# A delta-rule slot rearranged: the block substitution split around k S's part, VectorE's and ScalarE's rows in another order, GpSimd's long operations moved, G ahead of k'y

## The chip, the cores and the metric

The program runs on 1 core of a Trainium2 chip. The metric is the device time in microseconds of that core, from a run of the whole program; less is better. Before the change it is 2587.37 us (median of 3 runs, 2584.19 to 2587.85).

## The reference, cut to what matters

One step of a hybrid encoder layer: a projection, a gated delta rule with 8 heads (the part touched here), latent attention with 8 heads, and an output projection. 1024 prompt tokens and 32 sample tokens are processed, all in float32. The delta rule per chunk, with state `s`:

```python
lmat = where(strict, (k * beta) @ k.T * decay, 0)
tmat = triangular_solve(lmat + eye, eye)          # unit lower triangular
u = tmat @ (v * beta);  w = tmat @ (k * beta * exp(g))
attn = (q @ k.T) * decay
v_new = u - w @ s
o = (q * exp(g)) @ s + attn @ v_new
s = s * exp(g_last) + (k * exp(g_last - g)).T @ v_new
o_g = rmsnorm(o) * gdn_norm_w * silu(z_g)
```

## The kernel before, in words

The program has four stages that follow each other, each its own block: `project`, `delta_rule`, `attend`, `project_out`. Only `delta_rule` (span from about 1191 to 1626 us) is changed. It works on chunks of 128 tokens: chunks 0 to 7 are the prompt, chunk 8 (`LAST`) the sample, with its own state.

Each engine has its own instruction stream, written out by hand, and waits on semaphores (`Ledger.wait`). All streams run over the same slots: `each_slot` calls `slot(c)` for c from -2 to 9. In slot c the engines work on three chunks at once:

- chunk c+2, the early part: transposes of q and k (`qT`, `kT`), norms (`sse`, then `rs`, a power on GpSimd, then five small VectorE operations in `coefficients`: `kb`, `nlam`, `nle`, `sqc`, `sq2`), the decay matrix `D` from `gm_hi` and `gm_lo` (GpSimd, `growth`), its exponential `dL` and weighted copy `dLb` (ScalarE), the Gram matrix `G` (TensorE) and from them `lmat` (VectorE, `lower_products`, called L below).
- chunk c+1, the triangular solve: `substitute` on VectorE makes the inverses of 16x16 diagonal blocks, row by row: for i from 1 to 15 a product `m{i}` of `Lrep` and `x` and a reduction `x{i}`, each waiting for the one before. ScalarE expands `x` into `Y` (`Yx`), TensorE turns it (`X`), and `P4_`, `Y4_`, `X4_`, `P5_`, `Y5_`, `X5_`, `P6`, `Y6` join the blocks with the masks `C4` and `C5` (GpSimd).
- chunk c, the state: TensorE makes `kS`, `qS`, `y`, `dS`, `Ay`; VectorE adds into `R`, `qe`, the state `S` and the output `o`; ScalarE copies `y` and squares `o` (`osq`). GpSimd makes the decayed state `Sd`. Chunk c-1 is normalised (`orr`, `on` on GpSimd) and turned (`oT`), gated (`mix`) and stored.

`Lrep` is `lmat`'s diagonal blocks, repeated. It goes through DRAM: SyncE's `bounce(c+2)` waits for L, stores 8 blocks, waits for them, and loads 1024 KB back.

TensorE's results go to PSUM in pairs of banks. `PHASES` gives the order of TensorE's phases in a slot, and four pairs are handed out in turn: a phase takes the pair of the phase four places ahead of it, and `free` waits until that one's reader (`FREED`) is done.

`x13`, `m14` and so on are the rows of the substitution; in the rows of a trace their operations are told apart by size (`m{i}` has 8*i elements a partition, `x{i}` reads 8*(i+1)). `gdn_C` is C4 or C5, `gdn_o<-gdn_b,gates_eg` is qe, `gdn_o<-gdn_o,gdn_orr` is on.

Of the kernel before, what the change touches and what calls it, by code (L numbers as in the profile page):

```python
# [16 lines left out]
EPS = 1e-6  # L17
# [503 lines left out]
def delta_rule(nc, a, d, cols, ident, out, g_all, g_hi, g_lo, beta, eg, egl, edl):  # L521
# [4 lines left out]
    with ExitStack() as ctx:  # L526
# [134 lines left out]
        @block.gpsimd  # L661
        def _(pool):
            pool.memset(mhalf[:], -0.5).then_inc(set_up, 1)
            pool.memset(S[:, 0], 0.0).then_inc(set_up, 1)
            pool.wait_ge(set_up, 2)
            pool.wait_ge(consts_in, 16 * CONSTS)

            def mask(c, k, name, C):

                if k == 0:  # L670
                    DVE.wait(pool, c, "L1")
                PE.wait(pool, c - 1, f"P{4 + k}_1")
                POOL.done(pool.tensor_tensor(C[:], lmat[:, c % 2], level[:, k:k + 1, :].to_broadcast(full), ALU.mult), c, name)

            def growth(c, name, gm, g):

                PE.wait(pool, c - 1, "D1")
                POOL.done(pool.tensor_tensor(gm[:], lower[:, None, :].to_broadcast(full), g[:, c, :, None].to_broadcast(full), ALU.mult), c, name)

            def slot(c, live):  # L680
                if live(c + 1):
                    mask(c + 1, 0, "C4", C4)
                if live(c - 1):
                    DVE.wait(pool, c - 1, "orr")
# [8 lines left out]
                if live(c):  # L693
                    DVE.wait(pool, c - 1, "S1")
                    POOL.done(pool.tensor_tensor(Sd[:], S[:, stream(c)], egl[:, c, :, None].to_broadcast(full), ALU.mult), c, "Sd")
                if live(c + 2):
                    DVE.wait(pool, c + 2, "sse")
                    POOL.done(pool.tensor_tensor(rs[:], sse[:], mhalf[:], ALU.pow), c + 2, "rs")
# [12 lines left out]
        def _(act):
# [54 lines left out]
            def slot(c, live):  # L766
# [61 lines left out]
        def _(dve):  # L828
# [40 lines left out]
            def substitute(c, rows):  # L869

                for i in rows:
# [7 lines left out]
                    DVE.done(dve.tensor_reduce(x[:, :, i:i + 1].rearrange("p h o -> p (h o)"), prod[:, :, AT[i]:AT[i] + i + 1], AX.X, ALU.add), c, f"x{i}")  # L879

            def slot(c, live):
                if live(c):
                    POOL.wait(dve, c, "Sd") if c == 0 else None
# [40 lines left out]
                if live(c):  # L924
                    ACTS.wait(dve, c, "osq")
                    DVE.done(dve.tensor_tensor(var[:], oss[:], sq2[:, c], ALU.mult), c, "var0")
                    own(c, "var0")
                    DVE.done(dve.tensor_scalar(var[:], var[:], EPS, None, ALU.add), c, "var")
# [18 lines left out]
        def _(pe):  # L947
# [39 lines left out]
            def slot(c, live):  # L987
# [1130 lines left out]
```

## Time and profile before

| what | value |
|---|---|
| median of 3 runs | 2587.37 us |
| the profiled execution, its own time | 2585.61 us |
| its span | 2583.8 us |
| PE busy in the span | 2347.6 us (91%) |
| DVE, ACT, POOL busy | 1051.7, 746.8, 463.0 us |
| delta rule, slots 0 to 7 | 1269.25 to 1597.95 us of the span |

Times are microseconds from the start of the span. A row of the timeline gives the start, the length and the count of merged instructions; the bracket gives how long the engine sat idle before it and what released it. A slot is counted here from the first weight load of `kS`, and "at 8.2" in a slot means 8.2 us after that.

### The profile page before, as it was taken

To read this page: it belongs to the slowest core of one execution; us is meant where nothing else is said; L and a number is where in the kernel's file an instruction comes from. 1 tells how busy PE (TensorE), PEld (TensorE's weight loads), DVE (VectorE), ACT (ScalarE), POOL (GpSimd) and SP (SyncE) were. 2 spreads that over 40 slices of the span, in tenths; PEclk is the share of its full clock that TensorE was granted. 3 is DMA by queue.
4 is the path that set the end of the run, shared out by engine and by line. 5 is a ranking of instruction groups with operands and counts; after the bars stand their busy time and mean duration, and the time that the engine had idled before them with its cause. 6 is when DMAs were issued, how large, how long until landed. Compare 5 with 4: busy or idle time off the path is not lost. (4 is left out here: it accounts for less than half of the span.)

```text
span 2583.8 us, 37042 instructions
## 1 busy us (share of the span) xinstructions
PE 2347.6 (91%) x15280; PEld 2250.8 (87%) x15280; DVE 1051.7 (41%) x1743; ACT 746.8 (29%) x1860; POOL 463.0 (18%) x287
## 2 busy tenths in 40 slices
PE   6899999999999999995587878698999995999997
PEld 5899999999999999995587877597887874999997
DVE  3321345555545111110456565464444542334343
ACT  4111011111111111103456553323344341343343
POOL 1111222222212211112243543110000000111111
PEclk8999999999999999997799989799999998999999
DMA  5222122222222221213444422534222117858564
GB/s 159 71 75 75 50 75 75 66 67 66 75 75 75 75 75 60 74 50 93 88 91 94 108 51 60 172 125 116 58 59 88 56 43 244 248 144 253 150 186 128
DMA packets 328557, 257.72 MB, mean 100 GB/s; under 512 B 32533, under 2 KB 308326, under 8 KB 323942
## 3 DMA queue, kind: packets, MB, share of 16 engines
q1 hardware_dynamic: 300582, 219.33, 30.4%
q10 hardware_dynamic: 27808, 36.03, 3.8%
q8 instruction: 122, 2.00, 0.3%
q14 instruction: 45, 0.37, 0.0%
HBM read 192.42 MB, written 62.91 MB: 99 GB/s over the span
## 5 line engine op out<-in xcount | busy, mean ns | idle before, releaser
L457 PE MATMUL proj_acc<-proj_hn_hi,proj_w_hi 128*128 128x352 f32 (+1 forms) x2352 | 763.3, 325 | 7.0 <-DVE proj_hn_lo L338 6.0
L457 PE MATMUL proj_acc<-proj_hn_lo,proj_w_hi 128*128 128x352 f32 (+1 forms) x2352 | 755.6, 321 | 0.0
L457 PE MATMUL proj_acc<-proj_hn_hi,proj_w_lo 128*128 128x352 f32 (+1 forms) x2352 | 755.2, 321 | 0.0
L457 PEld LDWEIGHTS proj_acc<-proj_hn_hi,proj_w_hi 128*128 128x128 f32 (+1 forms) x2352 | 440.4, 187 | 8.8 <-issue 6.7
L457 PEld LDWEIGHTS proj_acc<-proj_hn_lo,proj_w_hi 128*128 128x128 f32 (+1 forms) x2352 | 441.3, 188 | 0.6
L457 PEld LDWEIGHTS proj_acc<-proj_hn_hi,proj_w_lo 128*128 128x128 f32 (+1 forms) x2352 | 440.1, 187 | 0.9
L2052 PE MATMUL mixo_acc<-mixo_m_hi,mixo_w_hi 128*128 128x384 f32 (+1 forms) x768 | 253.0, 329 | 31.6 <-DMA mixo_m_lo<-scratch_mix 21.6
L218 POOL TENSOR_TENSOR proj_w_raw<-proj_w_raw,all_cols 128x2048 f32<-128x2048 f32 (+1 forms) x49 | 175.7, 3586 | 420.3 <-DMA proj_w_raw<-in_w_in 420.3
L2052 PE MATMUL mixo_acc<-mixo_m_hi,mixo_w_lo 128*128 128x384 f32 (+1 forms) x768 | 248.7, 324 | 0.0
L2052 PE MATMUL mixo_acc<-mixo_m_lo,mixo_w_hi 128*128 128x384 f32 (+1 forms) x768 | 248.4, 323 | 0.0
L369 DVE TENSOR_TENSOR proj_act_out<-proj_acc,proj_rstd_b 128x352 f32<-128x352 f32 (+1 forms) x75 | 39.1, 524 | 365.9 <-PE proj_acc L457 353.4
L1990 DVE TENSOR_TENSOR mixo_w_lo<-mixo_w_raw,mixo_w_hi 128x2048 fp32r<-128x2048 f32 x48 | 110.0, 2292 | 175.2 <-ACT mixo_w_hi L1956 175.2
L343 DVE TENSOR_TENSOR proj_w_lo<-proj_w_raw,proj_w_hi 128x2048 fp32r<-128x2048 f32 (+1 forms) x49 | 111.5, 2276 | 162.1 <-ACT proj_w_hi L264 162.1
L2052 PEld LDWEIGHTS mixo_acc<-mixo_m_hi,mixo_w_hi 128*128 128x128 f32 x768 | 145.6, 190 | 34.1 <-DVE mixo_w_lo L1990 26.8
L380 DVE SCALAR_TENSOR_TENSOR proj_act_out<-proj_pre,all_cols,proj_act_out 128x1059 f32<-128x1059 f32 x72 | 172.7, 2399 | 2.5
L287 ACT ACTIVATE proj_act_out<-proj_act_out 128x1059 f32<-128x1059 f32 x24 | 26.2, 1090 | 474.6 <-DVE proj_act_out L380 474.6
L2052 PEld LDWEIGHTS mixo_acc<-mixo_m_lo,mixo_w_hi 128*128 128x128 f32 x768 | 145.9, 190 | 0.0
L2052 PEld LDWEIGHTS mixo_acc<-mixo_m_hi,mixo_w_lo 128*128 128x128 f32 x768 | 145.7, 190 | 0.0
L264 ACT CAST proj_w_hi<-proj_w_raw 128x2048 fp32r<-128x2048 f32 (+1 forms) x49 | 92.9, 1896 | 124.6 <-DVE proj_act_out L369 94.1
L365 DVE TENSOR_TENSOR proj_pre<-proj_acc,proj_rstd_b 128x352 f32<-128x352 f32 (+1 forms) x96 | 39.1, 429 | 182.4 <-PE proj_acc L457 179.9
L291 ACT ACTIVATE proj_act_out<-proj_act_out 128x1056 f32<-128x1056 f32 x16 | 17.4, 1087 | 305.0 <-DVE proj_act_out L369 305.0
L1956 ACT CAST mixo_w_hi<-mixo_w_raw 128x2048 fp32r<-128x2048 f32 x48 | 90.9, 1893 | 31.9 <-DMA mixo_w_raw<-in_w_out 31.7
(285 smaller groups left out, 3573.7 us busy)
## 6 DMA issues: line engine op xcount, KB each, us to landing
proj_w_raw<-in_w_in SPq DMA_DIRECT2D x48, 1024.0 KB, 5.7
mixo_w_raw<-in_w_out SPq DMA_DIRECT2D x48, 1024.0 KB, 6.1
scratch_qkv<-proj_act_out ACTq DMA_DIRECT2D x24, 529.5 KB, 2.8
gdn_qkv<-scratch_qkv SPq DMA_DIRECT2D x8, 1536.0 KB, 8.3
gdn_Lrep<-scratch_blocks SPq DMA_DIRECT2D x9, 1024.0 KB
scratch_gate<-proj_act_out ACTq DMA_DIRECT2D x16, 528.0 KB, 2.7
mixo_y<-in_x_prompt SPq DMA_DIRECT2D x8, 1024.0 KB, 9.1
out_y_prompt<-mixo_y SPq DMA_DIRECT2D x8, 1024.0 KB, 5.2
```

The source lines that it names most:

```text
L218: POOL.done(pool.tensor_tensor(w_raw[:, :, 0:n], w_raw[:, :, 0:n], cols[:, 0, R_LN:R_LN + KT][:, :, None].to_broadcast([P, KT, n]), ALU.mu ...
L264: ACTS.done(act.copy(w_hi[:, t % 2, :, 0:n], w_raw[:, :, 0:n]), t, "hi")
L287: ACTS.done(act.activation(act_out[:, b], act_out[:, b], ACT.Silu), j, "silu")
L291: ACTS.done(act.activation(act_out[:, b, 0:T], act_out[:, b, 0:T], ACT.Silu), QKV_TILES + j, "silu")
L343: DVE.done(dve.tensor_tensor(w_lo[:, t % 2, :, 0:n], w_raw[:, :, 0:n], w_hi[:, t % 2, :, 0:n].bitcast(F32), ALU.subtract), t, "lo")
L365: last = dve.tensor_tensor(pre[:, b, first + shift:end + shift], acc[b][c][:, first - NW * c:end - NW * c], rstd_b[:, first:end], ALU.mult)
L369: last = dve.tensor_tensor(act_out[0:n, b, cut(c)], acc[b][c][0:n, 0:NW], rstd_b[0:n, cut(c)], ALU.mult)
L380: DVE.done(dve.scalar_tensor_tensor(y, pre[:, b, n:n + CONV], w[n], y, ALU.mult, ALU.add), j, f"c{n}")
L457: last = pe.matmul(acc[b][c][0:n, 0:NW], w[:, b, k, 0:n], h[:, k, cut(c)], start=(k == 0 and i == 0), stop=(k == KT - 1 and i == 2))
L1956: ACTS.done(act.copy(w_hi[:, i % 2], w_raw[:, i % 2]), i, "hi")
L1990: DVE.done(dve.tensor_tensor(w_lo[:, i % 2], w_raw[:, i % 2], w_hi[:, i % 2].bitcast(F32), ALU.subtract), i, "lo")
L2052: last = pe.matmul(acc[i % 4][:, 0:n], w[:, i % 2, k], h[:, g % 2, k, 0:n], start=(k == 0 and x == 0), stop=(k == KT - 1 and x == 2))
```

## The change

Every operation stays; only places and waits move.

- VectorE: rows 1 to 7 of the substitution (chunk c+1) go ahead of `R`(c), rows 8 to 13 behind it, then `sse`, rows 14 and 15, `qe`, the coefficients. `o` goes ahead of L. The variance goes behind the first four additions of the solve. `S` waits for `Sd` once.
- GpSimd: the order in a slot is `rs`(c+2), `on`(c-1), C5(c+1), `gmh` and `gml`(c+3), (the memset), `Sd`(c+1), `mix_lo`(c-1), `orms`(c), C4(c+2). `on` also waits for row 15 of the substitution. `growth` and `Sd` are now made one slot earlier than they are used; chunk 0's `growth` stands ahead of the slots.
- ScalarE: `Yx` goes ahead of `dLb`; the copies of X and P4_ go ahead of the squares of o.
- TensorE: G goes ahead of dS. With `PHASES` changed in the same way, X takes the banks that G had (and so waits for L) and P4_ those that dS had (and waits for S); before it was the other way round.

```diff
-        PHASES = ["kS", "qT", "kT", "qS", "y", "D", "dS", "G", "Ay", "oT", "X", "P4_", "Y4_", "X4_", "P5_", "vT", "Y5_", "X5_", "A", "P6", "aT", "Y6"]
+        PHASES = ["kS", "qT", "kT", "qS", "y", "D", "G", "dS", "Ay", "oT", "X", "P4_", "Y4_", "X4_", "P5_", "vT", "Y5_", "X5_", "A", "P6", "aT", "Y6"]
...
@@ GpSimd
+            def both(c):
+                growth(c, "gmh", gm_hi, g_hi[:].bitcast(F32))
+                growth(c, "gml", gm_lo, g_lo[:])
+
             def slot(c, live):
-                if live(c + 1):
-                    mask(c + 1, 0, "C4", C4)
-                if live(c - 1):
-                    DVE.wait(pool, c - 1, "orr")
-                    POOL.done(pool.tensor_tensor(o[:, (c - 1) % 2], o[:, (c - 1) % 2], orr[:, :, None].to_broadcast(full), ALU.mult), c - 1, "on")
-                if live(c + 2):
-                    growth(c + 2, "gmh", gm_hi, g_hi[:].bitcast(F32))
-                    growth(c + 2, "gml", gm_lo, g_lo[:])
...
                 if live(c + 2):
                     DVE.wait(pool, c + 2, "sse")
                     POOL.done(pool.tensor_tensor(rs[:], sse[:], mhalf[:], ALU.pow), c + 2, "rs")
+                if live(c - 1):
+                    DVE.wait(pool, c - 1, "orr")
+                    if live(c + 1):
+                        DVE.wait(pool, c + 1, f"x{BASE - 1}")
+                    POOL.done(pool.tensor_tensor(o[:, (c - 1) % 2], o[:, (c - 1) % 2], orr[:, :, None].to_broadcast(full), ALU.mult), c - 1, "on")
                 if live(c + 1):
                     mask(c + 1, 1, "C5", C5)
+                if live(c + 3):
+                    both(c + 3)
...
+                if live(c + 1):
+                    DVE.wait(pool, c, "S1")
+                    POOL.done(pool.tensor_tensor(Sd[:], S[:, stream(c + 1)], egl[:, c + 1, :, None].to_broadcast(full), ALU.mult), c + 1, "Sd")
...
+                if live(c + 2):
+                    mask(c + 2, 0, "C4", C4)
+
+            both(0)
             each_slot(slot)
...
@@ ScalarE
+                if live(c + 1):
+                    expand(c + 1)
+                if live(c + 2):
                     DVE.wait(act, c + 2, "nlam")
...
                 if live(c + 1):
-                    expand(c + 1)
+                    PE.wait(act, c, "Y6")
+                    evacuate(c + 1, "X", X)
+                    PE.wait(act, c, "X5_1")
+                    evacuate(c + 1, "P4_", pc)
...
@@ VectorE
             def slot(c, live):
+                if live(c + 1):
+                    substitute(c + 1, range(1, BASE // 2))
                 if live(c):
...
+                if live(c + 1):
+                    substitute(c + 1, range(BASE // 2, BASE - 2))
                 if live(c + 2):
                     norms(c + 2)
+                if live(c + 1):
+                    substitute(c + 1, range(BASE - 2, BASE))
                 if live(c):
...
-                if live(c + 1):
-                    substitute(c + 1, range(1, BASE // 2))
                 if live(c + 2):
                     coefficients(c + 2)
-                if live(c + 1):
-                    substitute(c + 1, range(BASE // 2, BASE))
```

The engines' rows at three places. GpSimd in a middle slot before; the first row is C4 of chunk c+1, the second `on`, the third and fourth `growth` for c+2:

```order
L673 TENSOR_TENSOR gdn_C<-gdn_lmat,gdn_level 128x1024
L685 TENSOR_TENSOR gdn_o<-gdn_o,gdn_orr 128x1024
L678 TENSOR_TENSOR gdn_gm_hi<-gdn_lower,gates_g_hi 128x1024
L678 TENSOR_TENSOR gdn_gm_lo<-gdn_lower,gates_g_lo 128x1024
L695 TENSOR_TENSOR gdn_Sd<-gdn_S,gates_egl 128x1024
L698 TENSOR_TENSOR gdn_rs<-gdn_sse,gdn_mhalf 128x16
L673 TENSOR_TENSOR gdn_C<-gdn_lmat,gdn_level 128x1024
L703 TENSOR_TENSOR gdn_mix_lo<-gdn_mix,gdn_mix_hi 128x1024
L706 TENSOR_TENSOR gdn_orr<-gdn_var,gdn_mhalf 128x8
```

One long operation (C5) stands between `rs` and the wait for ScalarE's `mix_hi`. GpSimd in a middle slot now:

```order
L687 TENSOR_TENSOR gdn_rs<-gdn_sse,gdn_mhalf 128x16
L692 TENSOR_TENSOR gdn_o<-gdn_o,gdn_orr 128x1024
L673 TENSOR_TENSOR gdn_C<-gdn_lmat,gdn_level 128x1024
L678 TENSOR_TENSOR gdn_gm_hi<-gdn_lower,gates_g_hi 128x1024
L678 TENSOR_TENSOR gdn_gm_lo<-gdn_lower,gates_g_lo 128x1024
L703 TENSOR_TENSOR gdn_Sd<-gdn_S,gates_egl 128x1024
L706 TENSOR_TENSOR gdn_mix_lo<-gdn_mix,gdn_mix_hi 128x1024
L709 TENSOR_TENSOR gdn_orr<-gdn_var,gdn_mhalf 128x8
L673 TENSOR_TENSOR gdn_C<-gdn_lmat,gdn_level 128x1024
```

Four long operations follow `rs` now, ahead of the wait for the state in `Sd`. VectorE in the middle of the substitution before, around the five coefficients:

```order
L877 TENSOR_TENSOR gdn_prod<-gdn_Lrep,gdn_x 128x8x7
L879 TENSOR_REDUCE gdn_x<-gdn_prod 128x8
L849 TENSOR_TENSOR gdn_kb<-gdn_rs,gates_beta 128x8
L851 SCALAR_TENSOR_TENSOR gdn_nlam<-gdn_rs,gdn_kb 128x8
L853 TENSOR_TENSOR gdn_nle<-gdn_nlam,gates_eg 128x8
L854 TENSOR_SCALAR gdn_sqc<-gdn_rs 128x8
L856 SCALAR_TENSOR_TENSOR gdn_sq<-gdn_sqc 128x8
L877 TENSOR_TENSOR gdn_prod<-gdn_Lrep,gdn_x 128x8x8
```

The rows 8 to 15 of the substitution stand behind the coefficients, then S, L and o. VectorE from `sse` to S now:

```order
L852 TENSOR_SCALAR gdn_sse<-gdn_ssq 128x16
L884 TENSOR_TENSOR gdn_prod<-gdn_Lrep,gdn_x 128x8x14
L886 TENSOR_REDUCE gdn_x<-gdn_prod 128x8
L884 TENSOR_TENSOR gdn_prod<-gdn_Lrep,gdn_x 128x8x15
L886 TENSOR_REDUCE gdn_x<-gdn_prod 128x8
L915 TENSOR_TENSOR gdn_o<-gdn_b,gates_eg 128x512 x2
L856 TENSOR_TENSOR gdn_kb<-gdn_rs,gates_beta 128x8
L858 SCALAR_TENSOR_TENSOR gdn_nlam<-gdn_rs,gdn_kb 128x8
L860 TENSOR_TENSOR gdn_nle<-gdn_nlam,gates_eg 128x8
L861 TENSOR_SCALAR gdn_sqc<-gdn_rs 128x8
L863 SCALAR_TENSOR_TENSOR gdn_sq<-gdn_sqc 128x8
L922 TENSOR_TENSOR gdn_S<-gdn_Sd,gdn_b 128x512 x2
```

The substitution has ended when the coefficients come; S, o and then L stand behind them.

## Rows read from the trace of the kernel before

**Rows 1.** Groups by line and shape, delta rule: busy us, mean ns | idle before.

```profile
L678 POOL TENSOR_TENSOR gdn_gm_lo<-gdn_lower,gates_g_lo 128x1024 fp32r<-128x1024 f32 x9 | 17.1, 1899 | 0.0
```

**Rows 2.** Windows, slots 0, 3, 5 and 7: length, busy per engine, clock, DMA.

```profile
1269.25:1310.22 40.97, 34.22 (x288) 32.84 (x286) 23.58 (x65) 23.10 (x94) 11.39 (x6) 0.92 0.38 80
...
1394.07:1436.00 41.93, 35.57 (x296) 34.04 (x294) 24.90 (x67) 23.98 (x95) 18.97 (x10) 0.92 0.44 103
...
1478.00:1521.43 43.43, 35.58 (x296) 34.04 (x294) 26.39 (x67) 23.98 (x95) 20.96 (x11) 0.92 0.35 72
...
1563.35:1597.95 34.60, 29.39 (x258) 28.55 (x256) 21.15 (x59) 14.38 (x45) 10.01 (x6) 0.95 0.13 36
```

**Rows 3.** Timeline of slot 3: start, length, engine, line, operation [idle before].

```profile
1395.27 2.16 DVE L889 SCALAR_TENSOR_TENSOR gdn_R<-gdn_b,gdn_nle,gdn_R 128x128 f32<-128x128 f32 x8 [3.49 <-PE gdn_b L970]
...
1400.94 0.17 DVE L845 TENSOR_SCALAR gdn_sse<-gdn_ssq 128x16 f32<-128x16 f32 x1 [3.51 <-ACT gdn_sqT L734]
...
1401.19 2.91 POOL L698 TENSOR_TENSOR gdn_rs<-gdn_sse,gdn_mhalf 128x16 f32<-128x16 f32 x1 [1.87 <-DVE gdn_sse L845]
...
1404.06 2.36 POOL L673 TENSOR_TENSOR gdn_C<-gdn_lmat,gdn_level 128x1024 f32<-128x1024 f32 x1
...
1404.43 2.05 DVE L877 TENSOR_TENSOR gdn_prod<-gdn_Lrep,gdn_x 128x48 f32<-128x48 f32 x1
...
1412.46 1.27 DVE L908 TENSOR_TENSOR gdn_S<-gdn_Sd,gdn_b 128x512 f32<-128x512 f32 x2
...
1413.65 1.28 DVE L867 TENSOR_TENSOR gdn_lmat<-gdn_b,gdn_dLb 128x512 f32<-128x512 f32 x2
...
1415.07 1.57 PEld L976 LDWEIGHTS gdn_b<-all_ident,gdn_Y 128*128 128x128 f32 x8 [5.31 <-ACT gdn_Y L721]
...
1421.08 2.02 PE L970 MATMUL gdn_b<-gdn_pc,gdn_X 128*128 128x128 f32 x16 [0.62 <-ACT gdn_pc L758]
1421.29 0.62 SPq L645 DMA_DIRECT2D gdn_Lrep<-scratch_blocks  x1
...
1433.56 0.16 DVE L942 TENSOR_TENSOR gdn_orr<-gdn_orr,gdn_sqc 128x8 f32<-128x8 f32 x1
```

**Rows 4.** Timeline, projection stage: a long GpSimd operation beside VectorE's first of three.

```profile
340.34 3.61 POOL L218 TENSOR_TENSOR proj_w_raw<-proj_w_raw,all_cols 128x2048 f32<-128x2048 f32 x1
343.89 1.22 POOL L236 COPY proj_pre<-all_cols 128x3 f32<-128x3 f32 x1
...
340.37 4.69 DVE L380 SCALAR_TENSOR_TENSOR proj_act_out<-proj_pre,all_cols,proj_act_out 128x1059 f32<-128x1059 f32 x1
```

**Rows 5.** By source line, that VectorE operation: least, median, greatest ns.

```profile
L380 DVE SCALAR_TENSOR_TENSOR proj_act_out<-proj_pre,all_cols,proj_act_out x72: 1321/1323/4694, 294.6 to 827.1; 128x1059 f32<-128x1059 f32 x72
```

**Rows 6.** Timeline of slot 5, where C5 meets the first coefficient.

```profile
1490.36 2.36 POOL L673 TENSOR_TENSOR gdn_C<-gdn_lmat,gdn_level 128x1024 f32<-128x1024 f32 x1
...
1490.49 2.25 DVE L849 TENSOR_TENSOR gdn_kb<-gdn_rs,gates_beta 128x8 f32<-128x8 f32 x1
```

**Rows 7.** Timeline of slot -1: the first Lrep and an undisturbed substitution.

```profile
1224.61 0.67 SPq L645 DMA_DIRECT2D gdn_Lrep<-scratch_blocks  x1
...
1238.86 0.17 DVE L877 TENSOR_TENSOR gdn_prod<-gdn_Lrep,gdn_x 128x8 f32<-128x8 f32 x1 [16.41 <-DMA gdn_Lrep<-scratch_blocks]
...
1241.96 0.16 DVE L849 TENSOR_TENSOR gdn_kb<-gdn_rs,gates_beta 128x8 f32<-128x8 f32 x1
...
1242.72 0.22 DVE L877 TENSOR_TENSOR gdn_prod<-gdn_Lrep,gdn_x 128x64 f32<-128x64 f32 x1
...
1246.11 0.28 DVE L877 TENSOR_TENSOR gdn_prod<-gdn_Lrep,gdn_x 128x112 f32<-128x112 f32 x1
```

**Rows 8.** The page, DMA issues: KB each, median us from issue to landing.

```profile
gdn_qkv<-scratch_qkv SPq DMA_DIRECT2D x8, 1536.0 KB, 8.3
...
gdn_gate<-scratch_gate SPq DMA_DIRECT2D x8, 512.0 KB, 13.6
```

**Rows 9.** Timeline of slot -1: TensorE's Y4_ of chunk 0.

```profile
1254.33 2.01 PE L970 MATMUL gdn_b<-gdn_pc,gdn_X 128*128 128x128 f32 x16
```

More of the change, by code:

```diff
@@ L570, in delta_rule @@
                      state=two("R", "qe", "S", "o") + ["var0", "var"], scale=["orr"], tail=two("mix"))
-        POOL = Ledger(s, "pool", early=["gmh", "gml", "rs"], solve=["C4", "C5"], state=["Sd", "orms"], tail=["on", "mix_lo"])
+        POOL = Ledger(s, "pool", early=["gmh", "gml", "rs"], solve=["C4", "C5"], decayed=["Sd"], state=["orms"], tail=["on", "mix_lo"])
         consts_in, set_up, rounded, sample_padded, ssm_out = (
@@ L678, in growth @@
                 POOL.done(pool.tensor_tensor(gm[:], lower[:, None, :].to_broadcast(full), g[:, c, :, None].to_broadcast(full), ALU.mult), c, name)
+            def both(c):
+                growth(c, "gmh", gm_hi, g_hi[:].bitcast(F32))
+                growth(c, "gml", gm_lo, g_lo[:])
             def slot(c, live):
-                if live(c + 1):
-                    mask(c + 1, 0, "C4", C4)
+                if live(c + 2):
+                    DVE.wait(pool, c + 2, "sse")
+                    POOL.done(pool.tensor_tensor(rs[:], sse[:], mhalf[:], ALU.pow), c + 2, "rs")
                 if live(c - 1):
                     DVE.wait(pool, c - 1, "orr")
+                    if live(c + 1):
+                        DVE.wait(pool, c + 1, f"x{BASE - 1}")
                     POOL.done(pool.tensor_tensor(o[:, (c - 1) % 2], o[:, (c - 1) % 2], orr[:, :, None].to_broadcast(full), ALU.mult), c - 1, "on")
-                if live(c + 2):
-                    growth(c + 2, "gmh", gm_hi, g_hi[:].bitcast(F32))
-                    growth(c + 2, "gml", gm_lo, g_lo[:])
+                if live(c + 1):
+                    mask(c + 1, 1, "C5", C5)
+                if live(c + 3):
+                    both(c + 3)
                 if c + 3 == LAST:
@@ L692, in slot @@
                     pool.memset(qkv[:, LAST % 3, :, DEC:], 0.0).then_inc(sample_padded, 1)
[L693 to L698, printed above, removed]
                 if live(c + 1):
-                    mask(c + 1, 1, "C5", C5)
+                    DVE.wait(pool, c, "S1")
+                    POOL.done(pool.tensor_tensor(Sd[:], S[:, stream(c + 1)], egl[:, c + 1, :, None].to_broadcast(full), ALU.mult), c + 1, "Sd")
                 if live(c - 1):
@@ L777, in slot @@
                         ACTS.done(act.activation(dL[:, (c + 2) % 2, half(g)], bank(at("D", c + 2, g)), ACT.Exp), c + 2, f"dL{g}")
+                if live(c + 1):
+                    expand(c + 1)
+                if live(c + 2):
                     DVE.wait(act, c + 2, "nlam")
@@ L793, in slot @@
                     ACTS.done(last, c, "osq")
-                if live(c + 1):
-                    PE.wait(act, c, "Y6")
-                    evacuate(c + 1, "X", X)
                 if live(c - 1):
@@ L802, in slot @@
                 if live(c + 1):
-                    PE.wait(act, c, "X5_1")
-                    evacuate(c + 1, "P4_", pc)
                     PE.wait(act, c + 1, "X4_1")
@@ L879, in substitute, with variance @@
                     DVE.done(dve.tensor_reduce(x[:, :, i:i + 1].rearrange("p h o -> p (h o)"), prod[:, :, AT[i]:AT[i] + i + 1], AX.X, ALU.add), c, f"x{i}")
+            def variance(c):
+                ACTS.wait(dve, c, "osq")
+                DVE.done(dve.tensor_tensor(var[:], oss[:], sq2[:, c], ALU.mult), c, "var0")
+                own(c, "var0")
+                DVE.done(dve.tensor_scalar(var[:], var[:], EPS, None, ALU.add), c, "var")
             def slot(c, live):
+                if live(c + 1):
+                    substitute(c + 1, range(1, BASE // 2))
                 if live(c):
-                    POOL.wait(dve, c, "Sd") if c == 0 else None
                     for g in G2:
@@ L915, in slot @@
                         DVE.done(dve.tensor_tensor(o[:, c % 2, half(g)], o[:, c % 2, half(g)], bank(at("Ay", c, g)), ALU.add), c, f"o{g}")
+                if live(c + 2):
+                    lower_products(c + 2)
                 if live(c - 1):
@@ L923, in slot @@
                                                           gate[:, (c - 1) % 2, half(g)], ALU.mult, ALU.mult), c - 1, f"mix{g}")
[L924 to L928, printed above, removed]
                 if live(c + 1):
@@ L932, in slot @@
                     add(c + 1, "X4_", X)
+                if live(c):
+                    variance(c)
+                if live(c + 1):
                     add(c + 1, "Y5_", Y[:, (c + 1) % 2], "Y4_")
@@ L1013, in slot @@
                         PE.done(pe.matmul(bank(at("D", f, g)), ident_r[:], neg_r[:, None, :].to_broadcast([P, HF, P]), start=False, stop=True), f, f"D{g}")
+                if far:
+                    for g in G2:
+                        heads("G", f, part(f, 1), part(f, 1), g)
                 if now:
@@ L1016, in slot @@
                         heads("dS", c, kd[:, c % 3], y, g, [(ACTS, c, f"y{g}"), (ACTS, c, "kd1")])
-                if far:
-                    for g in G2:
-                        heads("G", f, part(f, 1), part(f, 1), g)
                 if now:
```

6 lines of the change are left out of this document (1 added, 5 removed).

## The prediction

> **What bounds the kernel now.** I read the page (TensorE busy for 91% of the span), then windows cut at the slots of the delta rule, then one slot in order of time. Slots 0, 3, 5 and 7 took 40.97, 41.93, 43.43 and 34.60 us [rows 2]; slots 1, 2, 4 and 6 lie within 0.1 us of slot 3.
>
> In slot 3, starting at 1394.07, TensorE works almost without a gap except before X, where its loads wait 5.31 us for ScalarE's Yx, until 1415.07, at 21.0 in the slot [rows 3]. Yx waits for the last row of the substitution, which is over when S starts, at 18.4. The substitution stands behind R, a wait of 3.51 us for ScalarE's squares and qe, and one product of it takes 2.05 us where its neighbours take 0.2: it starts while GpSimd's C5 runs (1404.06 + 2.36) and ends with it [rows 3]. A smaller wait is 0.62 us ahead of Y4_ [rows 3]. So the time of a slot is when X can start, plus the 20.9 us from there to the next slot.
>
> **What the change takes away.** Undisturbed, rows 1 to 7 take 3.10 us (1238.86 to 1241.96) and rows 8 to 13 take 3.39 (1242.72 to 1246.11) [rows 7]; rows 14 and 15 take about 1.2. Let m1 start at a in its slot. R is then at a+3.1 (not before 1.2, as now), 2.16 long; row 13 is done at a+8.65, and the substitution at about a+10. Even with a = 0 that is 8 us earlier than now, and Yx (2.4 us, ScalarE) no longer holds X: TensorE reaches X's place at about 15. The copies of X and P4_ ahead of osq remove the 0.62 us ahead of Y4_, and P4_'s first copy starts earlier: I take 0.8 us less from X to the next slot, so 20.1. G ahead of dS saves nothing while X waits later.
>
> **What comes in its place.** GpSimd now has on, C5, gmh, gml one behind the other after rs, all with their inputs ready, and VectorE's five coefficients need rs too. The trace shows two things. A GpSimd operation over SBUF and a VectorE one with two SBUF inputs run one after the other: kb, behind C5 by 0.13 us, took 2.25 us and ended with it [rows 6], and the GpSimd operation behind rs starts before VectorE's. And where both have a next one, they take turns: VectorE's first operation, normally 1.32 us [rows 5], waited out the 3.61 us one and went ahead of GpSimd's COPY, which was behind it; that took 1.22 us for 3 elements, having waited for VectorE's, although VectorE had two more [rows 4]. So kb waits for on, nlam (which needs kb) for C5, nle for gmh, sqc or sq2 for gml. Each hand-over costs a long operation: on, gmh and gml have one shape and last 1.90 us [rows 1], C5 2.36 [rows 3]. Sum 3x1.90 + 2.36 + about 0.4 for what the small ones add = 8.5 us where the five took 0.76 (1241.96 to 1242.72) [rows 7]. No row shows four in a chain; bounds are 0.8 us (none meets) and 9.5 us (each of five waits). I take 8.5, as both single cases are shown.
>
> The Trainium skill, "SBUF — State Buffer", section "Who interferes with whom", says the same of a VectorE instruction with two SBUF inputs against a GpSimd one that reads SBUF: the second to come is fully blocked. It speaks against the move, and the trace agrees (2.05 and 2.25 us). By it alone the order of turns is open.
>
> Behind the coefficients stand S, o and L, 1.19 us from one pair to the next (1412.46 to 1413.65 [rows 3]), and X now needs the banks that L reads. rs is done 3.1 us after sse, so at T = a+8.65+3.1 = a+11.8, not before 10.0 (sse at 6.87 now, bound by the squares). X starts at T + 8.5 + 2x1.19 + 0.8 = T+11.7, and L ends 0.6 us behind that.
>
> What is a? m1 may follow orr (1433.56, 2.5 us ahead of the slot's end), but it needs Lrep. From the end of L (1414.93) to Lrep's issue (1421.29) are 6.4 us [rows 3]. Its landing has no row of its own. From above it is 14.25 us, the first one's, with a 1536 KB load beside it (1224.61 to 1238.86 [rows 7]). From below it is 5.5, the rate of the qkv load (1536 KB in 8.3 us) [rows 8]. gate, 512 KB, is issued 0.67 us behind Lrep and lands 13.6 us later [rows 8], 14.3 in all; with some 2 us of that its own I take 12.3. So L to m1 is 18.7 us (11.9 to 20.7). Until now 8 us of slack hid it; now the cover is gone.
>
> **A middle slot.** X at s gives a slot of s+20.1, L ends at s+0.6, the next m1 is at s+0.6+18.7-(s+20.1) = -0.8. Then T = 11.0, X at 22.7, the slot 42.8: 0.9 us more than 41.93. The wait of TensorE moves from Yx (until 21.0) to L (until 22.7). Later in the slot nothing binds: the variance waits for GpSimd's mix_lo, but Y5_'s addition comes after that.
>
> **Slot by slot.**
> - Slot -2: kb and nlam meet gmh and gml of chunk 1, so L(0), Lrep(0) and m1(0) come 2.8 us later. Slot -1: rs(1) now stands behind row 13 rather than ahead of m1, and C5, gmh, gml and Sd follow it: L(1) ends about 12 us later. dLb waits for nlam and stands ahead of X's copy on ScalarE, so Y4_ starts at about 1260 rather than 1254.33 [rows 9]: +5.7 together.
> - Slot 0: Lrep(1) lands at 4.5, R waits behind m1 to m7: 43.8 against 40.97, +2.8.
> - Slot 1: a = 1.4, the slot 45.0, +3.1.
> - Slots 2 to 4: 3 x 0.8 = +2.4 (a slot being 42.7 to 42.8).
> - Slot 5: 42.8 against 43.43 (the memset no longer holds rs), -0.6.
> - Slot 6: no gmh and gml, so the coefficients take 5.0: -2.6.
> - Slot 7: no coefficients, so X at about 12 (substitution at 9, on 1.9, oT 0.9), and 20.1 behind it less some 1.3, as no long wait lets TensorE's clock fall (its mean of 0.95 [rows 2] is 3.5 us at half): 30.8 against 34.60, -3.8.
>
> Sum +7.0 us. The profiled execution took 2585.61, so 2592.6; the median of the runs is 1.8 above the profiled one, so 2594.
>
> **Rivals.**
>
> *VectorE gets its small operations through behind on alone* (the coefficients end 2.7 us after T). For it: the small ones last 0.16 us and follow 0.2 us apart. Against it: GpSimd's COPY went in between two VectorE operations without any gap [rows 4]. L would end at a+18.1; the loop through Lrep is 18.1+18.7 = 36.8 a slot, -5.1 in each of slots 1 to 5 (26), -7 in slot 6, -3.8 in slot 7, +3.0-1.8 at the start: -34 to -36, 2552. This is the one on the other side: not slower but 1.3% faster. It decides as soon as the coefficients take under about 6.5 us. 14%.
>
> *Lrep lands early.* With 15 us or less from L to m1, a is held by orr (-2.3) and T by the squares (10.0): X at 21.7, slots of 41.8, so nothing gained in the middle; slots 0 and 1 lose nothing, 5, 6 and 7 give 9 back, less the 5.7: about -4, 2583. 22%.
>
> *Lrep lands late* (20.7 us): a = +1.0, slots of 44.7, +22 in all: 2609. 16%.
>
> *The banks or the port are no matter and PE is full:* slots bound by TensorE alone (36 or less): 2545 to 2550. It would need Lrep early and no turns. 5%.
>
> **How the numbers follow.** The forecast, 2594, has 43%; its own range, with Lrep's bounds, is 2583 to 2610. Two executions of this kernel can be told apart from about 0.2% (5 us). Faster by more than that: the first and last rival, 19%, and 5% of the early-landing case: 24%. Within: the rest of that case and the lower part of the forecast's, 25%. Slower: 51%. The range, 2554 to 2609, leaves out the fastest cases and a little above.
>
> **What the profile after would show.** Right: kb, nlam, nle and sqc or sq2 with lengths near 2 us in slots 1 to 5; no product of the substitution above 0.3 us; X's idle time released by DVE's lmat and not by Yx, 6 to 8 us long; m1 idle for DMA's Lrep by 1 to 2 us in middle slots and by several in slots 0 and 1; slots of 42 to 43.5. Wrong: coefficients that end within 4 us after rs (then the kernel is faster); m1 right behind orr in every slot (Lrep early); X still released by Yx; or a wait for `on` ahead of oT that nothing here counts.

## The result and the profile after

The changed kernel takes 2595.54 us (median; 2588.67 to 2598.54), the kernel before 2587.85 us in the same series. The ratio is 1.003, 95% interval 1.0017 to 1.0043: slower by 0.3%, 1.5 us above the forecast of 2594. The profiled span is 2594.9 us, at a mean granted clock of 0.956 (before 2583.8 and 0.958).

The stretches are again cut where the weight loads of k S start. Windows of the profile after, slots 0, 1, 3, 5 and 7; the columns are those of [rows 2]: stretch, length, busy time (and count) of TensorE's matmuls, its weight loads, VectorE, ScalarE and GpSimd, granted clock, DMA share, GB/s.

```profile
1276.72:1319.97 43.25, 36.04 (x288) 34.72 (x286) 27.05 (x65) 23.27 (x94) 14.79 (x7) 0.88 0.37 79
1319.97:1362.71 42.74, 34.51 (x296) 33.41 (x294) 31.81 (x67) 24.13 (x95) 19.01 (x9) 0.92 0.35 76
1406.46:1450.27 43.81, 35.55 (x296) 34.44 (x294) 31.83 (x67) 24.26 (x95) 19.01 (x9) 0.88 0.43 101
1492.40:1536.57 44.17, 34.99 (x296) 33.71 (x294) 31.86 (x67) 24.26 (x95) 20.92 (x10) 0.92 0.36 72
1576.98:1607.39 30.41, 28.18 (x258) 27.30 (x256) 22.78 (x59) 14.65 (x45) 11.98 (x6) 1.00 0.15 43
```

Slots 2, 4 and 6 took 43.75, 42.13 and 40.41 us. VectorE is busy for 31.8 us in a middle slot where it was 24.9, with the same 67 instructions: 7 us are instructions that stand and wait. The eight slots together are 2.0 us longer than before, and slot 0 starts 7.5 us later. The other 1.6 us by which the two profiled spans differ lie outside this stretch.

Timeline of slot 1 after, from `sse` to the next Lrep (start, length, engine, line, operation [idle before]):

```profile
1329.23 0.17 DVE L852 TENSOR_SCALAR gdn_sse<-gdn_ssq 128x16 f32<-128x16 f32 x1
1329.47 2.91 POOL L687 TENSOR_TENSOR gdn_rs<-gdn_sse,gdn_mhalf 128x16 f32<-128x16 f32 x1 [15.57 <-DVE gdn_sse L852]
...
1332.35 1.89 POOL L692 TENSOR_TENSOR gdn_o<-gdn_o,gdn_orr 128x1024 f32<-128x1024 f32 x1
1332.41 1.85 DVE L856 TENSOR_TENSOR gdn_kb<-gdn_rs,gates_beta 128x8 f32<-128x8 f32 x1 [0.65 <-POOL gdn_rs L687]
...
1334.20 2.35 POOL L673 TENSOR_TENSOR gdn_C<-gdn_lmat,gdn_level 128x1024 f32<-128x1024 f32 x1
1334.30 2.28 DVE L858 SCALAR_TENSOR_TENSOR gdn_nlam<-gdn_rs,gdn_kb 128x8 f32<-128x8 f32 x1
...
1336.52 1.89 POOL L678 TENSOR_TENSOR gdn_gm_hi<-gdn_lower,gates_g_hi 128x1024 fp32r<-128x1024 f32 x1
1336.62 1.82 DVE L860 TENSOR_TENSOR gdn_nle<-gdn_nlam,gates_eg 128x8 f32<-128x8 f32 x1
1338.36 0.16 DVE L861 TENSOR_SCALAR gdn_sqc<-gdn_rs 128x8 f32<-128x8 f32 x1
1338.37 1.90 POOL L678 TENSOR_TENSOR gdn_gm_lo<-gdn_lower,gates_g_lo 128x1024 fp32r<-128x1024 f32 x1
1338.55 1.74 DVE L863 SCALAR_TENSOR_TENSOR gdn_sq<-gdn_sqc 128x8 f32<-128x8 f32 x1
1340.21 1.27 DVE L922 TENSOR_TENSOR gdn_S<-gdn_Sd,gdn_b 128x512 f32<-128x512 f32 x2
...
1342.60 1.28 DVE L874 TENSOR_TENSOR gdn_lmat<-gdn_b,gdn_dLb 128x512 f32<-128x512 f32 x2
1343.40 1.57 PEld L987 LDWEIGHTS gdn_b<-all_ident,gdn_Y 128*128 128x128 f32 x8 [7.63 <-issue]
...
1350.67 0.62 SPq L645 DMA_DIRECT2D gdn_Lrep<-scratch_blocks  x1
```

Each of the four long GpSimd operations behind `rs` has one coefficient beside it that ends with it: kb with `on`, nlam with C5, nle with `gm_hi`, sq2 with `gm_lo`; only sqc passes. The coefficients end at 1340.29, 7.9 us behind `rs`, where the five took 0.76 [rows 7]. X, which waited 5.31 us for Yx [rows 3], waits 7.63 us for L (the weight load's row says "issue"; its matmul's row, at 1343.43, names `lmat`). By source line, all nine of three of the coefficients (least, median, greatest ns):

```profile
L856 DVE TENSOR_TENSOR gdn_kb<-gdn_rs,gates_beta x9: 1849/1851/2310, 1213.1 to 1549.9; 128x8 f32<-128x8 f32 x9
L858 DVE SCALAR_TENSOR_TENSOR gdn_nlam<-gdn_rs,gdn_kb x9: 1817/2278/2282, 1215.0 to 1551.7; 128x8 f32<-128x8 f32 x9
L863 DVE SCALAR_TENSOR_TENSOR gdn_sq<-gdn_sqc x9: 167/1742/1744, 1217.2 to 1554.3; 128x8 f32<-128x8 f32 x9
```

The page's waits after say where the loop holds the engines, L ahead of X and Lrep ahead of the substitution (engine, what it wanted, line, who released it: us in total, times, longest):

```profile
PE gdn_b L987 <- DVE gdn_lmat L874: 41.3, 6, 7.4
```

```profile
DVE gdn_prod L884 <- DMA gdn_Lrep<-scratch_blocks: 49.7, 9, 21.0
```

Before, of the first products of the nine chunks only chunk 0's waited for Lrep (16.41 us [rows 7]); now all nine do.

### The profile page after: what moved, and what is told of

Read it like the earlier page. It is cut to its first block and busy times, and to the rows that moved or that the text cites. A ratio compares the mean times of both kernels' runs of the same rounds, so it can differ in the third digit from the quotient of the medians.

```text
span 2594.9 us, 37040 instructions
## 1 busy us (share of the span) xinstructions
PE 2348.9 (91%) x15280; PEld 2253.8 (87%) x15280; DVE 1103.4 (43%) x1743; ACT 747.9 (29%) x1860; POOL 463.2 (18%) x287
```

## The experiments

Each is timed against the kernel before on the same chip. Experiments 1 to 5, 9 and 11 are one edit each to the changed kernel, to experiment 1 or to the kernel before; 6, 7, 8 and 10 build on the ones that their headings name. The ratio's 95% interval stands in brackets.

**1. The changed kernel with GpSimd's long operations held until the coefficients are done.**

```diff
                     POOL.done(pool.tensor_tensor(rs[:], sse[:], mhalf[:], ALU.pow), c + 2, "rs")
+                    DVE.wait(pool, c + 2, "sq2")
```

> The changed kernel with one wait more: GpSimd waits for the last coefficient (sq2 of chunk c+2) behind rs, so that on, C5, gmh and gml cannot meet the five. Theory (VectorE and GpSimd take turns at SBUF): kb, nlam, nle, sq2 fall from about 1.8 to 2.3 us each to 0.16, the coefficients end 1 us after rs instead of 8.5, L 7.5 us earlier; then the loop m1 to L to Lrep to m1 sets the slot: 16.4 + 19.7 = 36 to 37 us in slots 1 to 5 against 42.1 to 44.2; 2553 to 2562 us in all. Rival (the banks of X, or Lrep alone, set the slot and the port does not matter): slots of 42 to 44 stay, 2594 to 2597.

Measured: 2553.29 us, ratio 0.9871 [0.9854, 0.9887]. One wait more makes the kernel 42 us faster, which is the fast end of what was expected. Timeline of its slot 3:

```profile
1389.32 2.91 POOL L687 TENSOR_TENSOR gdn_rs<-gdn_sse,gdn_mhalf 128x16 f32<-128x16 f32 x1 [15.76 <-DVE gdn_sse L853]
...
1392.27 0.17 DVE L857 TENSOR_TENSOR gdn_kb<-gdn_rs,gates_beta 128x8 f32<-128x8 f32 x1 [0.65 <-POOL gdn_rs L687]
...
1392.96 0.17 DVE L864 SCALAR_TENSOR_TENSOR gdn_sq<-gdn_sqc 128x8 f32<-128x8 f32 x1
1393.04 1.28 DVE L923 TENSOR_TENSOR gdn_S<-gdn_Sd,gdn_b 128x512 f32<-128x512 f32 x2
1393.20 1.90 POOL L693 TENSOR_TENSOR gdn_o<-gdn_o,gdn_orr 128x1024 f32<-128x1024 f32 x1 [0.97 <-DVE gdn_sq L864]
```

The five take 0.86 us, GpSimd loses 0.97 us, and the slots 1 to 5 are 35.4 to 36.5 us. The loop still binds there: the first product waits 4.1 to 5.2 us for Lrep. The window of slot 3 (as [rows 2]) shows that TensorE's clock comes back too, from 0.88 to 1.00; with it PE's busy time falls from 35.55 to 33.58 us:

```profile
1378.24:1414.68 36.44, 33.58 (x297) 31.95 (x296) 24.87 (x67) 24.40 (x96) 19.02 (x9) 1.00 0.53 120
```

**2. The same wait, but for nlam only**, so that two of the five still meet a long operation.

```diff
+                    DVE.wait(pool, c + 2, "nlam")
```

> The changed kernel with GpSimd waiting for the second coefficient (nlam) instead of the last. Theory (one hand-over for each VectorE operation with two SBUF inputs): nle meets on (1.85 us), sq2 meets C5 (2.3), coefficients end 4.8 us behind rs, between 1.0 (wait for sq2) and 7.9 (no wait): slots near 40, 2572 to 2580 us. Rival (only the start of a GpSimd operation beside kb and nlam matters, or the wait works by holding on back): as with the wait for sq2, 2553.

Measured: 2574.83 us, 0.9948 [0.9932, 0.9964], inside the range; slots 1 to 5 are 38.9 to 40.4. The cost grows with the number of coefficients that meet a long operation: none, two and four go with slots of about 36, 40 and 43. Which two was expected wrongly: nle had started 0.04 us ahead of `on` and took 0.17 us. Its slot 3 also shows the one that passed before, sqc, held like the others once it comes behind the start of `on`:

```profile
1408.51 1.90 POOL L693 TENSOR_TENSOR gdn_o<-gdn_o,gdn_orr 128x1024 f32<-128x1024 f32 x1 [0.48 <-DVE gdn_nlam L859]
1408.55 1.88 DVE L862 TENSOR_SCALAR gdn_sqc<-gdn_rs 128x8 f32<-128x8 f32 x1
1410.37 2.35 POOL L673 TENSOR_TENSOR gdn_C<-gdn_lmat,gdn_level 128x1024 f32<-128x1024 f32 x1
1410.47 2.27 DVE L864 SCALAR_TENSOR_TENSOR gdn_sq<-gdn_sqc 128x8 f32<-128x8 f32 x1
```

**3. GpSimd's part of the change alone**, in the kernel before.

```diff
-                if live(c + 1):
-                    mask(c + 1, 0, "C4", C4)
                 ... (the whole GpSimd part of the diff)
+                if live(c + 2):
+                    mask(c + 2, 0, "C4", C4)
```

> The kernel before with GpSimd's part of the change alone. Theory: the product that took 2.05 us takes 0.2, the substitution ends at 16.6 in the slot instead of 18.4, then on (1.9) holds oT, and X starts at 19.4 instead of 21.0: slots of 40.3 against 41.9, 2575 to 2579 us. Rival (GpSimd's order is no matter by itself, VectorE's order does it all): slots of 41.9, 2586 to 2589.

Measured: 2579.78 us, 0.9969 [0.9957, 0.998], 0.8 us above the expected range. The middle slots are 40.1 as expected, but the way to slot 0 is 4 us longer and slot 0 itself 3, which the expectation left out. The coefficients are through before `on` here (kb 0.16 us at 1408.83), since `on` waits for the last row of the substitution, behind them. The bound is now that wait:

```profile
1414.35 1.90 POOL L692 TENSOR_TENSOR gdn_o<-gdn_o,gdn_orr 128x1024 f32<-128x1024 f32 x1 [6.73 <-DVE gdn_x L885]
...
1416.30 1.57 PEld L982 LDWEIGHTS gdn_b<-all_ident,gdn_o 128*128 128x128 f32 x8 [3.85 <-POOL gdn_o L692]
```

**4. The changed kernel with GpSimd's order of before.**

```diff
+                if live(c + 1):
+                    mask(c + 1, 0, "C4", C4)
                 ... (the GpSimd part of the diff undone)
-                if live(c + 2):
-                    mask(c + 2, 0, "C4", C4)
```

> The changed kernel with GpSimd's order of before (on, gmh, gml, Sd at the slot's start; rs, C5 behind). Theory: gmh, gml and Sd now meet products 1 to 3 of the substitution (+3.4 us), C5 alone meets kb (coefficients end 3.1 us behind rs): m1 to L 22.0, plus 19.7 through DRAM, slots of 41.7 against 43.7: 2580 to 2590 us. Rival (what costs is the new order of VectorE, TensorE and banks, not where GpSimd's operations are): slots of 43 to 44, 2594 to 2597.

Measured: 2577.24 us, 0.9959 [0.9945, 0.9974], 2.8 us below the expected range; slots 41.3 (0.4 below expectation; slot 4 is 39.8), and the start is not late (slot 0 at 1269.38). Only C5 stands behind `rs`, so kb alone is held (2.31 us), but the first products of the substitution meet `gm_hi`, `gm_lo` and `Sd`, timeline of slot 3:

```profile
1393.38 0.78 DVE L878 TENSOR_TENSOR gdn_prod<-gdn_Lrep,gdn_x 128x8 f32<-128x8 f32 x1 [3.09 <-DMA gdn_Lrep<-scratch_blocks]
...
1394.39 1.62 DVE L878 TENSOR_TENSOR gdn_prod<-gdn_Lrep,gdn_x 128x16 f32<-128x16 f32 x1
...
1396.26 1.61 DVE L878 TENSOR_TENSOR gdn_prod<-gdn_Lrep,gdn_x 128x24 f32<-128x24 f32 x1
```

So either half of the change gains about 0.3 to 0.4% alone, and both together lose 0.3%. In experiment 3 row 15 of the substitution comes behind the coefficients, so `on`, which waits for it, and the row behind `on` come too late to meet them. The early substitution takes that cover away: `on` can start as soon as `rs` is done, just when the coefficients do.

**5. The changed kernel with G behind dS again** (X then has dS's banks and P4_ those of G).

```diff
-        PHASES = [..., "D", "G", "dS", "Ay", ...
+        PHASES = [..., "D", "dS", "G", "Ay", ...
```

> The changed kernel with G behind dS again, in the code and in the list that hands out banks: X waits for S, P4_ for L. Theory (the loop from L through Lrep to m1 to L sets the slot, 24.0 + 19.7): X starts about 2 us earlier in the slot, m1 about as much later, the slot stays 43 to 44: 2593 to 2597 us. Rival (the loss is that X waits for L's banks): slots 1.5 to 2 us shorter, 2583 to 2588.

Measured: 2596.28 us, 1.0032 [1.0019, 1.0045], the time of the changed kernel. X waits 3.7 to 5.5 us in slots 1 to 5 instead of 7.6, and y up to 3.7 us instead: which banks X takes moves the wait and doesn't change the slot (slots 0 to 5 are 43.1 us on average, 43.3 in the changed kernel). The loop through L and Lrep sets it, with m1 waiting for Lrep in each of them.

**6. Experiment 1, with L ahead of o.**

```diff
+                if live(c + 2):
+                    lower_products(c + 2)
                 if live(c):
                     for g in G2:
                         PE.wait(dve, c, f"Ay{g}")
...
-                if live(c + 2):
-                    lower_products(c + 2)
```

> The kernel with the wait for sq2, and L ahead of o on VectorE. Theory (the loop L, blocks to DRAM, Lrep, m1, L sets the slot there, m1 being idle 5.2 us for Lrep): L ends 0.95 us earlier (bound then by dLb), slots of 35.5 instead of 36.4: 2545 to 2550 us. Rival (TensorE is full in those slots, apart from what the order of o and L costs it): 2552 to 2555.

Measured: 2551.33 us, 0.9861 [0.9847, 0.9875], 1.3 us above the expected range and 0.7 below the rival's. The two intervals overlap with those of experiment 1, so the gain of 2 us is not clear of the noise. Slots 3 to 5 are 0.5 to 0.9 us shorter than there, slots 1 and 2 are not.

**7. Experiment 6, with `sse` right behind R.**

```diff
+                if live(c + 2):
+                    norms(c + 2)
                 if live(c + 1):
                     substitute(c + 1, range(BASE // 2, BASE - 2))
-                if live(c + 2):
-                    norms(c + 2)
```

> As the one with L ahead of o, and sse right behind R, ahead of rows 8 to 13, so that rs runs under them. Theory: the coefficients come 0.6 us earlier and L with them, another 0.6 us a slot: 2541 to 2547 us. Rival (rs was hidden): no change against the one with L ahead of o.

Measured: 2546.61 us, 0.9843 [0.983, 0.9856], inside the range. The mechanism isn't shown by it: 0.6 us a slot was expected, and slots 1 to 5 fell by 0.2 us on average. Of the 4.1 us between the two profiled spans 1.5 us lie ahead of slot 0 and 2.2 behind slot 7.

**8. Experiment 7, with Lrep in two halves**, rows 0 to 7 and 8 to 15, each with its own semaphore.

```diff
-                sp.dma_start(Lrep[:], blocks_d[c % 2]....to_broadcast([NB, BASE, BASE * HEADS * BASE])).then_inc(blocks_in, 16)
+                for rows, sem in ((slice(0, MID), blocks_in), (slice(MID, BASE), blocks_in2)):
+                    sp.dma_start(Lrep[:, rows], ....to_broadcast([NB, BASE, MID * HEADS * BASE])).then_inc(sem, 16)
...
+                        if i == MID:
+                            dve.wait_ge(blocks_in2, 16 * (c + 1))
```

> As the one with sse behind R, and Lrep loaded in two halves, rows 0 to 7 first, each with its own semaphore; row 8 waits for the second. Theory (Lrep's landing holds m1, R behind it and y): the first half lands some 6 us earlier, m1 follows orr at once, R is no longer late, TensorE is nearly full: slots of 34.2 to 34.5, 2536 to 2542 us. Rival (the DRAM path is latency and queueing, so half a load lands no earlier, or the second half holds row 8): no gain or a loss, 2544 or more.

Measured: 2523.31 us, 0.9755 [0.9741, 0.9768], 13 us better than the expectation. The middle slots fall to 34.5 us and no product in them waits for Lrep. Slot 6, which was 44.7 to 45.8 us in experiments 1, 6 and 7, is 37.4: that was missing in the expectation. The trace of experiment 6 shows why slot 6 was long. From its timeline, GpSimd and SP in slot 5 and the first product of chunk 7:

```profile
1471.63 2.03 POOL L701 MEMSET gdn_qkv<- 128x2304 f32 x1
...
1473.74 0.37 SPq L628 DMA_DIRECT2D gdn_qkv<-scratch_qkv  x1
1474.20 7.40 SPq L642 DMA_DIRECT2D scratch_blocks<-gdn_lmat  x8
...
1482.87 0.63 SPq L645 DMA_DIRECT2D gdn_Lrep<-scratch_blocks  x1
...
1496.23 0.17 DVE L885 TENSOR_TENSOR gdn_prod<-gdn_Lrep,gdn_x 128x8 f32<-128x8 f32 x1 [14.24 <-DMA gdn_Lrep<-scratch_blocks]
```

The memset stands behind four long operations. SP's load of the last chunk waits for it, and the blocks of chunk 7, whose L ended at 1466.62, stand behind that load in SP's queue until 1474.20. The whole Lrep then took 13.4 us more; its first half takes 7.0 in experiment 8, and slot 6 is 7.8 us shorter there than in experiment 7. The start gives 5.3 us (slot 0 at 1264.41 for 1269.70), slot 7 another 4.6; slots 0 to 5, where the gain was expected, give 6.0 together.

**9. Experiment 1, with the memset right behind `rs`**, ahead of the wait for sq2.

```diff
+                if c + 3 == LAST:
+                    PE.wait(pool, LAST - 3, "qS1")
+                    pool.memset(qkv[:, LAST % 3, :, DEC:], 0.0).then_inc(sample_padded, 1)
...
-                if c + 3 == LAST:
```

> The run with VectorE's wait for sq2 (sq2 awaited behind rs), with one more move: GpSimd's memset of the padded samples stands right behind rs, ahead of its wait for sq2, instead of behind on, C5, gmh and gml. Theory: slot 6 is 44.65 us long there, against 36.4 for its neighbours, because in slot 5 the memset comes late, SP's load of chunk 8 waits for it, and bounce(7), queued behind that load on SP, brings Lrep some 9 us late for the first product of chunk 7. Then slot 6 falls to about 36 us, slot 5 stays at about 35.5, and the kernel takes 2553.3 - 9 = 2544 us (2542 to 2548). Rival: slot 6 is long for another reason (chunk 8's conv work or TensorE's own queue); then slot 6 stays at 44 us and the time at 2553 us.

Measured: 2546.44 us, 0.9842 [0.9827, 0.9857]: 6.9 us less than experiment 1. Slot 6 falls from 44.65 to 36.49 us, so the cause of its length is shown; slot 5 rises from 35.93 to 37.79, which was not expected. (The wait for sq2 that the expectation names is GpSimd's, for a result of VectorE.) SP in slot 5:

```profile
1468.23 0.37 SPq L628 DMA_DIRECT2D gdn_qkv<-scratch_qkv  x1
1472.01 5.74 SPq L642 DMA_DIRECT2D scratch_blocks<-gdn_lmat  x8
1479.02 0.62 SPq L645 DMA_DIRECT2D gdn_Lrep<-scratch_blocks  x1
```

**10. Experiment 8 with `sse` back behind row 13 and the memset early**, the best version that this study found.

```diff
                 if live(c + 1):
                     substitute(c + 1, range(BASE // 2, BASE - 2))
+                if live(c + 2):
+                    norms(c + 2)
                 ... (and the memset as in experiment 9)
```

> The kernel with Lrep in halves, L ahead of o and VectorE's wait for sq2, with two more moves: sse stands back behind the product of row 13 (so rows 8 to 13 no longer wait behind it for the squares), and the memset stands right behind rs. Theory: dS's wait of 1.9 us for sse's bank goes from each middle slot (34.5 to about 32.8) and slot 6 loses about 3 us: 2523.3 - 7 x 1.7 - 3 = about 2508 us (2505 to 2515). Rival: TensorE's own queue is full at 34.5 us a slot, so the wait of dS only moves elsewhere and slot 6 alone gains: 2520 us (2517 to 2523).

Measured: 2513.85 us (2512.8 to 2515.76), ratio 0.9721 [0.9707, 0.9734], within the range but at its slow end. The wait of dS (1.93 us in experiment 8) is gone, yet the slots fell by 0.9 us only, to 33.6, since X now waits for L twice, 0.46 and 0.69 us; slot 6 is 33.6 too. A middle slot:

```profile
1363.10:1396.67 33.57, 32.87 (x296) 31.70 (x294) 25.20 (x68) 24.03 (x95) 19.02 (x9) 1.00 0.55 128
```

TensorE is busy for 32.87 of the 33.57 us at the full clock: it is nearly the bound.

**11. The kernel before with Lrep in halves only.**

```diff
+                for rows, sem in ((slice(0, MID), blocks_in), (slice(MID, BASE), blocks_in2)):
                 ... (as in experiment 8)
```

> The kernel before, with one edit: Lrep comes in two halves, each with its own semaphore, and the product of row 8 waits for the second. Theory: Lrep's landing binds only where the turns at SBUF have stretched the way to the blocks, or where everything else is short; in the kernel before Lrep has about 8 us of slack in a middle slot, so the slots stay at 41.9 us and only the first product, which waited 16.4 us, comes earlier: kernel 2580 to 2588 us. Rival: Lrep's landing limits the kernel before too; then the middle slots fall by 1 us or more each and the kernel takes 2578 us or less.

Measured: 2580.63 us, 0.9976 [0.9968, 0.9985]. The slots are those of before (41.13, 41.91, 41.93, ..., 43.43, 41.91, 34.67); the gain that the trace shows is the first product, earlier by about 7 us, which brings slot 0 from 1269.25 to 1264.92. The first product (8 elements) and that of row 8 (64 elements) of chunk 0:

```profile
1231.89 0.18 DVE L882 TENSOR_TENSOR gdn_prod<-gdn_Lrep,gdn_x 128x8 f32<-128x8 f32 x1 [8.77 <-DMA gdn_Lrep<-scratch_blocks]
...
1237.59 0.23 DVE L882 TENSOR_TENSOR gdn_prod<-gdn_Lrep,gdn_x 128x64 f32<-128x64 f32 x1 [1.75 <-DMA gdn_Lrep<-scratch_blocks]
```

So Lrep's landing has cover in the kernel before, as the prediction said.

## Why the prediction was right, step by step

**What the change takes away**: right. The substitution no longer stands behind R: in slot 1 it is over at 10.6 in the slot (before at 18.4), the products last 174 to 285 ns with none of 2 us, and X no longer waits for Yx in any middle slot.

**The turns at SBUF**: right, and shown by intervention. The prediction had each coefficient with two SBUF inputs wait out one long operation, kb `on`, nlam C5, nle `gm_hi`, and "sqc or sq2" `gm_lo`; it was sq2. Forecast 8.5 us from `rs` to the end, measured 7.9. What the estimate had too much is the 0.4 us added for the small ones and about 0.2 us by which the records of successive operations overlap. Experiment 1 takes only the meeting away and gets 42 us; experiment 2 gives part of it back. The rival in which VectorE gets its small ones through behind `on` falls by the nine lengths of nlam. What it priced, 2552 us, is what experiment 1 reached (2553), where the coefficients are through ahead of `on`: the price was right and its condition was not.

That the second to come is blocked is what the Trainium skill, "SBUF — State Buffer", section "Who interferes with whom", says of a VectorE instruction with two SBUF inputs against a GpSimd one that reads SBUF, and the trace agrees (kb 1.85 us beside `on`). The order of turns comes from the traces alone.

**The loop through L and Lrep**: right in kind. Experiment 5 excludes that the banks under X set the slot. In slots 1 to 5 the trace has 22.6 us from m1 to X (forecast 23.5: `sse` comes 0.2 us earlier, the coefficients 0.6) and 20.4 to 21.5 us from X to the next m1 (forecast 19.3).

**Where the size was off.** Three terms, which partly cancel, so that the 1.5 us between forecast and result are in part luck:

- *Lrep's landing*, taken as 12.3 us between 5.5 and 14.25, is 12.5 to 13.6 us in slots 0 to 6 (for example from 1350.67 to 1364.07, 13.4). With up to 1.8 us more than forecast from L's end to the issue, m1 comes at 0.2 to 2.2 us in its slot and not at −0.8, and slots 2 to 5 are 42.1 to 44.2 us where 42.8 was forecast. From L's end to m1 it was 19.9 to 21.0 us (m1 in slots 2 to 6) where 18.7 was forecast: the path was about as long as in the rival "Lrep lands late" (20.7 us, 2609 in all). That the kernel didn't take 2609 is due to the 0.9 us less from m1 to X, to up to 0.8 us less from X to the next slot, and to slots 0 and 1. (By the prediction's own terms that rival has m1 at +1.2 and slots of 44.8 us; it wrote +1.0 and 44.7.)
- *The way to slot 0* was taken as +5.7 us and is +7.5. Y4_ of chunk 0 starts at 1258.96, 4.6 us later than [rows 9] (forecast 5.7). But the clock, which the term left out, is lower there: TensorE waited 29.6 us ahead of X and 3.09 us ahead of Y4_, and from there to P5_, the next phase that reads Y, it runs at a granted clock of 0.54, near the lower level of 1.2 GHz. Before, it waited 19.8 us ahead of X, had 0.59 from X to Y4_ (1249.86 to 1254.33) and 1.00 from Y4_ on. Windows of after and, in the second fence, of before, from Y4_ to P5_:

```profile
1258.96:1265.44 6.48, 6.47 (x32) 6.48 (x33) 2.97 (x5) 0.39 (x1) 2.36 (x1) 0.54 0.10 9
```

```profile
1254.33:1257.97 3.64, 3.64 (x35) 3.64 (x33) 2.06 (x3) 0.59 (x1) 3.32 (x2) 1.00 0.16 25
```

  The same work takes 2.8 us more: 4.6 + 2.8 = 7.4, all of the start's delay.
- *Slots 0 and 1* were given +2.8 and +3.1 us; they are +2.3 and +0.8. Lrep(1) landed 3.1 us into slot 0 where 4.5 was taken. In slot 1, m1 came at 0.8 rather than 1.4 us, and from X to the next slot it took 19.3 us where 20.1 was taken, at a granted clock of 0.91 (in slot 3 it took 20.2 us, at 0.86).

Slots 2 to 4 were forecast at +2.4 together and are +3.8; slot 5 at −0.6 and is +0.7; slot 6 at −2.6 and is −1.5; slot 7 at −3.8 and is −4.2 (its clock is 1.00, as forecast). The sum of the profiled stretch is +9.4 us, forecast +7.0; the medians differ by 7.7. Of the signs that the prediction named, m1's wait for Lrep was too small: 1 to 2 us in middle slots, measured 2.5 to 4.5.

**The banks or the port are no matter** (2545 to 2550) had 5% and was wrong for this kernel, though its price is about what experiment 9 takes (2546). That is not its mechanism: in experiment 9 the first product of a middle slot still waits 4.3 to 5.4 us for Lrep.

**What the prediction didn't see** is how near the better kernel was: it treated the order of GpSimd's work as given. The one wait of experiment 1 follows from its own sum of turns.

## What to carry to other kernels

Short operations of VectorE over SBUF that many wait for should not be issued while GpSimd has a row of long ones ready: a wait on GpSimd that costs it 1 us a slot took 42 us off the kernel. Follow a loop of the kernel all the way through its DMA (here L, blocks, Lrep, substitution) before pricing a move, since the cover of a transfer goes as soon as one part of the loop grows, and ask what stands in the queue of an issuing engine behind a load that waits. Two moves that each gain alone (0.3 and 0.4%) can lose together, so a change of several parts is worth timing by its parts.

## What the runs showed of the hardware

- VectorE and GpSimd, both with SBUF operations ready, took strict turns by whole operations: four operations of 8 elements a partition, 0.17 us each alone, cost 1.85, 2.28, 1.82 and 1.74 us, about the length of the one with 1024 elements beside it. GpSimd's own lengths don't change (1.89, 2.35, 1.89, 1.90).
- An operation of VectorE with one SBUF tensor as input wasn't exempt: sqc, a multiplication by a constant, took 0.16 us when it came 0.01 us ahead of `gm_lo`, and 1.88 us when it came 0.04 us behind the start of `on` (experiment 2). The first operation of the variance, with two inputs, takes 2.0 to 2.1 us beside `mix_lo` in the changed kernel and 0.17 in the kernel before, where it does not meet it.
- Of two transfers of half the size, issued 0.7 us apart, the first is there 6.6 us after its issue (experiment 11, 1225.28 to 1231.89) and 7.0 us (experiment 8 in slot 5, 1468.24 to 1475.22), the second 12.3 us after the first one's issue (experiment 11, 1237.59); the whole took 12.5 to 14.5 us in the changed kernel. The projection's loads of 1024 KB land in 5.7 us (median, page of the profile before); why Lrep takes twice as long no run here tested.
- Slots 1 to 5 of experiment 1, where no wait of TensorE is over 2 us, have a granted clock of 1.00; those of the changed kernel, with a wait of 7.6 us each, have 0.88 to 0.92, and TensorE's busy time is 0.9 to 2.0 us more for the same instructions. In these kernels such a wait is thus paid for once more.
